# Collecting the second layer's expert results and the double norm behind it: one stage, tile by tile, instead of two

## What is computed

```python
        hn = rms_norm(h, norm_ffn[i])
        h = h + hier_moe(hn, ...)          # sum of two gated expert rows per token
    return rms_norm(h, norm_final)         # end of the first network, x of the second
...
    h, hc = x, ctx
    for layer in range(DEPTH):
        ...
        u = rms_norm_2(h, norm_g[layer]) * (1 + scale) + shift
        uc = rms_norm_2(hc, norm_g[layer]) * (1 + scale_c) + shift_c
```

## Time and profile before

| what | value |
|---|---|
| median of three runs | 3350.32 us |
| profiled execution: device time, span | 3346.29 us, 3344.5 us |
| TensorE busy | 2847.3 us, 85% of the span |
| VectorE, ScalarE, GpSimd busy | 839.7 us (25%), 643.0 (19%), 192.8 (6%) |
| mean granted TensorE clock | 0.949 of 2.4 GHz |
| collecting stage with the context's norm | about 2135.4 to 2154.0 us |
| double norm | 2154.0 to 2185.4 us |
| mixer A's products | 2185.5 to about 2306 us |

### The profile page before, as it was taken

One profiled execution on the slowest core, in us unless ns is written; L12 is line 12 of the kernel. 1 busy time (PEld: TensorE's weight loads), 2 busy tenths in 40 slices (PEclk: granted clock), 3 DMA queues, 4 the chain that ended last, 5 costly groups with the idle time before them and its releaser, 6 DMA issues. The chain is left out here.

```text
span 3344.5 us, 30732 instructions
## 1 busy us (share of the span) xinstructions
PE 2847.3 (85%) x12394; PEld 1426.5 (43%) x12394; DVE 839.7 (25%) x2159; ACT 643.0 (19%) x1388; POOL 192.8 (6%) x144
## 2 busy tenths in 40 slices
PE   7999949778867999998588777489999997999997
PEld 3454533222223444444332222146655564555554
DVE  1130421101102202112211110323714443054044
ACT  2220410000001000001000000213503342142143
POOL 1000010000000000000100000110010102012001
PEclk9999959999998999998699999799999998999999
DMA  5502059999984333224699999701001011121100
GB/s 186 232 26 76 26 216 380 427 427 427 428 335 170 125 115 112 101 75 176 244 428 427 427 427 428 277 25 34 1 27 39 13 51 48 51 73 48 51 23 32
DMA packets 117647, 604.84 MB, mean 181 GB/s; under 512 B 9701, under 2 KB 23978, under 8 KB 92794
## 3 DMA queue, kind: packets, MB, share of 16 engines
q1 hardware_dynamic: 91632, 537.15, 39.8%
q10 hardware_dynamic: 20618, 46.89, 4.0%
q0 software_dynamic: 5248, 18.75, 1.5%
HBM read 559.17 MB, written 43.52 MB: 180 GB/s over the span
## 5 line engine op out<-in xcount | busy, mean ns | idle before, releaser
L479 PE MATMUL psum<-ring,XT 128*128 128x512 f32 (+3 forms) x1216 | 480.2, 555 | 14.7 <-ACT arena L1705 6.6
L469 PE MATMUL psum<-XT,ring 128*128 128x512 f32 (+1 forms) x1152 | 444.2, 547 | 2.8 <-DVEq L2078 2.8
L1061 PE MATMUL psum<-arena 128*64 128x512 f32 x1280 | 306.1, 624 | 114.0 <-DMA arena<-in_expert_w_gu 113.8
L479 PEld LDWEIGHTS psum<-ring,XT 128*128 128x128 f32 x1216 | 230.2, 190 | 256.4 <-issue 222.4
L469 PEld LDWEIGHTS psum<-XT,ring 128*128 128x128 f32 x1152 | 219.3, 191 | 226.8 <-issue 215.6
L561 PE MATMUL psum<-ring,arena 128*128 128x512 f32 x704 | 306.1, 593 | 8.5 <-DVEq L2078 4.2
L1061 PE MATMUL psum<-ring,arena 128*64 128x512 f32 x768 | 191.5, 646 | 70.0 <-DMA ring<-in_expert_w_gu 67.2
L686 PE MATMUL psum<-arena 64*128 64x384 f32 (+8 forms) x704 | 221.1, 500 | 27.1 <-ACT arena L740 22.1
L1061 PEld LDWEIGHTS psum<-arena 128*64 128x64 f32 x1280 | 91.5, 142 | 300.2 <-issue 172.9
L1131 DVE TENSOR_TENSOR arena<-arena,psum 64x512 f32<-64x512 f32 x64 | 44.1, 689 | 692.4 <-ACT arena L1134 692.4
L561 PEld LDWEIGHTS psum<-ring,arena 128*128 128x128 f32 x704 | 132.2, 190 | 171.9 <-issue 159.3
(11 more groups left out here) (246 smaller groups left out, 2323.5 us busy)
## 6 DMA issues: line engine op xcount, KB each, us to landing
arena<-in_expert_w_gu SPq DMA_DIRECT2D x80, 2048.0 KB, 24.7
ring<-in_expert_w_gu SPq DMA_DIRECT2D x48, 2048.0 KB, 24.6
arena<-in_expert_w_down SPq DMA_DIRECT2D x40, 2048.0 KB, 28.1
ring<-in_expert_w_down SPq DMA_DIRECT2D x24, 2048.0 KB, 28.1
ring<-in_ada_w SPq DMA_DIRECT2D x12, 2048.0 KB, 9.3
ring<-in_fox_w_in SPq DMA_DIRECT2D x8, 2048.0 KB, 8.4
arena<-xg_dram ACTq DMA_DIRECT2D x32, 512.0 KB, 10.3
y_dram<-arena ACTq DMA_DIRECT2D x128, 128.0 KB, 8.6
```

The costliest lines, as they stand in the source:

```text
L469: i = pe.matmul(ps[0][0:cols_[1] - cols_[0], 0:ntok], w[:, c, cols_[0]:cols_[1]], x[:, c, tok:tok + ntok], start=(c == 0), stop=(c == k - 1))
L479: i = pe.matmul(ps[0][:, 0:width], x[:, c, t * P:(t + 1) * P], w[:, c, c0:c0 + width], start=(c == 0), stop=(c == k - 1))
L1061: i = pe.matmul(psum[side * BR:(side + 1) * BR, 0:FF], x[:, 4 * part + c, :], w[:, c, side * FF:(side + 1) * FF], start=(part == 0 and c = ...
```

## The change

The two stages become one, `CombineNorms`, for the second layer; the first layer keeps `Combine`. The load of norm_final comes first on ScalarE. VectorE adds a tile's two gathered rows and at once makes its Z; ScalarE takes both sums of squares of each tile as they come, all eight. The roots are as before. TensorE transposes the rows in two passes, tiles 0 and 1 of all banks, then tiles 2 and 3. GpSimd clears mixer A's query halves behind the gathers and then scales H. The places of Z, ROWS, G, the scratch rows and the context's norm in the arena are other ones. Mixer A's products have no clears any more, and a slack towards GpSimd.

```diff
+        class CombineNorms(Combine):
+            Z, ROWS = region(2 * NT * D, NT, D), region(NT * D, NT, D)
+            G, JUNK = region(21504, D), region(22528, D)
+            ZEROS = [region(12288, 8, NTA * P)[(1 - g) * DH:(2 - g) * DH, 4 * g:4 * g + 4, :] for g in range(2)]
...
+            def act(self, act):
+                act.dma_start(self.G, io["norm_final"].partition_broadcast(P)).then_inc(self.s("gain"), 16)
+                self.beside.act(act)
+                for t in range(NT):
+                    act.wait_ge(self.s("summed"), t + 1)
+                    act_step.then(act, act.activation(self.JUNK, H[:, t, :], ACT.Square, accum_out=s2[:, 0, t:t + 1]))
+                    act.wait_ge(self.s("weighted"), t + 1)
+                    i = act.activation(self.JUNK, self.Z[:, t, :], ACT.Square, accum_out=s2[:, 0, NT + t:NT + t + 1])
+                    if t + 1 < NT:
+                        act_step.then(act, i)
+                i.then_inc(self.s("squares"), 1)
...
+            def dve(self, dve):
+                self.beside.dve(dve)
+                dve.wait_ge(self.s("gain"), 16)
+                for t in range(NT):
+                    dve.wait_ge(self.s(f"got{t}"), self.at(f"got{t}") + 32)
+                    for k in range(2):
+                        i = dve.scalar_tensor_tensor(H[:, t, :], self.YG[:, k, t, :], gates[:, k, t:t + 1], H[:, t, :], ALU.mult, ALU.add)
+                        if k == 0:
+                            dve_step.then(dve, i)
+                    i.then_inc(self.s("summed"), 1)
+                    dve.wait_ge(self.s("summed"), t + 1)
+                    dve.tensor_tensor(self.Z[:, t, :], H[:, t, :], self.G, ALU.mult).then_inc(self.s("weighted"), 1)
+                dve.wait_ge(self.s("weighted"), NT)
+                dve.wait_ge(self.s("squares"), 1)
...
+            def pool(self, pool):
+                super().pool(pool)
+                for x in self.ZEROS:
+                    pool_step.then(pool, pool.memset(x, 0.0))
+                pool.wait_ge(self.s("rstd"), 1)
+                for t in range(NT):
+                    pool.tensor_scalar(H[:, t, :], self.Z[:, t, :], s2[:, 1, t:t + 1], None, ALU.mult)
+
+            def pe(self, pe):
+                self.beside.pe(pe)
+                pe.wait_ge(self.beside.s("out_a"), self.beside.at("out_a") + KC)
+                for t0 in range(0, NT, 2):
+                    pe.wait_ge(self.s("rows_a"), t0 // 2 + 1)
+                    pe.wait_ge(self.s("rows_v"), t0 // 2 + 1)
+                    for c in range(KC):
+                        for t in range(t0, t0 + 2):
+                            i = pe.transpose(bank(c)[:, t * P:(t + 1) * P], self.ROWS[:, t, c * P:(c + 1) * P], ident)
+                        if t0 + 2 == NT:
+                            i.then_inc(self.s("turned"), 1)
...
-            combine = Combine(f"cb{layer}")
+            combine = (CombineNorms if layer else Combine)(f"cb{layer}")
             if layer:
                 combine.beside = Norm("m01", HC, D, NCT, lambda c: amod[:, 0, c, 1:2], lambda c: modc[:, 0, c, 1:2], XT, SEQ,
-                                      region(2 * NT * D, NCT, D), side=1, junk=region(2 * NT * D + NCT * D, D)).inline()
+                                      region(18432, NCT, D), side=1, junk=region(18432 + NCT * D, D)).inline()
...
-        class TwoNorms(Stage):
...
-                for t in range(NT):
-                    i = act.activation(self.JUNK[:, 0, :], H[:, t, :], ACT.Square, accum_out=s2[:, 0, t:t + 1])
-                    act_step.then(act, i)
-                for t in range(0, NT, 2):
-                    act.wait_ge(self.s("weighted"), t + 1)
-                    i = act.activation(self.JUNK[:, 0, :], self.Z[:, t, :], ACT.Square, accum_out=s2[:, 0, NT + t:NT + t + 1])
...
-            zeros(p, *(QT[(1 - g) * DH:(2 - g) * DH, 4 * g:4 * g + 4, :] for g in range(2)))
+            p.slack = {(e, "pool"): 1 for e in ("pe", "act", "dve")}
...
-                 lambda: TwoNorms("nfin"), mixer_a, mixer_b,
+                 mixer_a, mixer_b,
```

More of the change, by code:

```diff
@@ L1240, in dve @@
                                                                     H[:, t, :], ALU.mult, ALU.add))
+        class CombineNorms(Combine):
+            Z, ROWS = region(2 * NT * D, NT, D), region(NT * D, NT, D)
+            G, JUNK = region(21504, D), region(22528, D)
+            ZEROS = [region(12288, 8, NTA * P)[(1 - g) * DH:(2 - g) * DH, 4 * g:4 * g + 4, :] for g in range(2)]
+            one, two = slice(0, NT), slice(NT, 2 * NT)
+            def act(self, act):
[9 more added lines that the diff above has]
+                i.then_inc(self.s("squares"), 1)
+                act.wait_ge(self.s("rstd"), 1)
+                for t in range(0, NT, 2):
+                    act.activation(self.ROWS[:, t, :], self.Z[:, t, :], ACT.Copy, scale=s2[:, 3, t:t + 1]).then_inc(self.s("rows_a"), 1)
+                for c in range(0, KC, 2):
+                    act.wait_ge(self.s("turned"), c + 1)
+                    act.activation(XT[:, c, 0:SEQ], bank(c), ACT.Identity, scale=amod[:, 0, c, 0:1], bias=modc[:, 0, c, 0:1])
+            def dve(self, dve):
[12 more added lines that the diff above has]
+                dve.wait_ge(self.s("squares"), 1)
+                dve_step.then(dve, dve.tensor_scalar(s2[:, 0, self.one], s2[:, 0, self.one], 1.0 / D, EPS, ALU.mult, ALU.add))
+                root_of(dve, *(s2[:, j, self.one] for j in (0, 2, 3, 1)))
+                r, ms = s2[:, 1, self.one], s2[:, 0, self.two]
+                dve_step.then(dve, dve.tensor_tensor(s2[:, 2, self.one], r, r, ALU.mult))
+                dve_step.then(dve, dve.tensor_tensor(ms, ms, s2[:, 2, self.one], ALU.mult))
+                dve_step.then(dve, dve.tensor_scalar(ms, ms, 1.0 / D, EPS, ALU.mult, ALU.add))
+                root_of(dve, *(s2[:, j, self.two] for j in (0, 2, 3, 1)))
+                dve.tensor_tensor(s2[:, 3, self.one], r, s2[:, 1, self.two], ALU.mult).then_inc(self.s("rstd"), 1)
+                dve.wait_ge(self.s("rstd"), 1)
+                for t in range(1, NT, 2):
+                    dve.tensor_scalar(self.ROWS[:, t, :], self.Z[:, t, :], s2[:, 3, t:t + 1], None, ALU.mult).then_inc(self.s("rows_v"), 1)
+                for c in range(1, KC, 2):
+                    dve.wait_ge(self.s("turned"), c + 1)
+                    dve.tensor_scalar(XT[:, c, 0:SEQ], bank(c), amod[:, 0, c, 0:1], modc[:, 0, c, 0:1], ALU.mult, ALU.add)
+            def pool(self, pool):
[16 more added lines that the diff above has]
+                            i.then_inc(self.s("turned"), 1)
@@ L1308, in loads @@
             stage.small = 16 * len(pairs)
[L1310 to L1315, removed]
         def gain_cols(at):
```

## The result

The changed kernel takes 3328.92 us in the median of seven runs (3325.95 to 3336.10), the kernel before, beside it, 3347.22 (3342.69 to 3352.61). The ratio is 0.9946, interval 0.9935 to 0.9957: 14 to 22 us faster. The forecast was 3337 with 3331 as the low end, so the way was right and the time lies outside the range.

The account below looks back on a forecast made before the run. The prediction took the two stages as a chain of waits, chiefly 7.35 us for a load and 3.5 for GpSimd. Gains of 8.4, 3.4 and 1.7 us made 13.5, from 3350.3 to 3336.8, said as 3337; range 3331 to 3344.

Parts of the forecast that it names:

- the seam: First gather to mixer A's seventeenth product, all that the change touches; the forecast gain summed to 13.5 us.
- Start of the tile sums: Joined stage: the early gain load pushes the gathers back 0.5 us, so VectorE's first sum starts at 2143.2.
- Tile loop: VectorE in the joined stage: two adds and one product per tile, 3.82 us each, four tiles 15.3 us.
- The end of the roots: End of the joined stage's two roots: 2164.8 instead of 2173.2, 8.4 us earlier.
- Clears beside the adds: GpSimd's two clears beside VectorE's adds in the joined stage: cost taken as 0, upper end 3.4 us.
- Rival B: Joined stage: clears hold VectorE 3.4 us, gathers delayed 1.4 more, clock falls 1.7; gain 7.0 us, 3343; chance 0.16.
- From the roots to the first product: Row scaling, transposes and copies up to mixer A: 8.9 us after the roots instead of 12.3.
- the split: Transposing in two passes of tile pairs ahead of mixer A brings nothing, because the copies to XT bound it.
- The clock at mixer A's start: TensorE's shorter idle gap keeps full clock over mixer A's first products: 1.7 us gained, lower end 0.
- rival C: Mixer A: TensorE's clock stays at 1.2 GHz, losing 25 us, 3363.5, slower; chance 0.03.
- The slack: Mixer A's products may start before GpSimd has finished scaling H: 3.4 us gained.
- Rival D: Something taken as free, such as a weight unit or GpSimd's queue, ends the chain: 3346, within 0.2%; chance 0.07.

Follow-up runs that it names:

- b_gain: The kernel before, two stages kept, with the load of norm_final issued at the head of the collecting stage; 0.9983 against the kernel before.
- a_onepass: The changed kernel with the transposes in one pass of four tiles to a bank, as before; 0.9963 against the kernel before.
- b_warm: The kernel before with 24 more transposes, results unread, on TensorE while GpSimd still scales H; 0.9986 against the kernel before.
- b_slack: The kernel before with mixer A's products given slack towards GpSimd and Z of the double norm moved; 0.9993 against the kernel before.
- b_delay: The kernel before with the first root's product with itself made eleven times, a 2.0 us delay; 1.0003 against the kernel before.
- a_best: The changed kernel with 40 filler transposes ahead of the rows and the first root ahead of Z's squares; 0.9948 against the kernel before.
- a_gainlate: The changed kernel with the load of norm_final issued behind the context's norm on ScalarE; 0.9981 against the kernel before.

## Why the prediction was wrong, and where it was right

The mechanism and nearly all terms of the seam were right; its sum was 13.5, and the traces show 13.9 in the first pair and 13.3 in the means. That these are so near is in part luck, since small misses of both signs cancel.

- *Start of the tile sums*: forecast 2143.2, found 2143.29, released by a gather. The agreement is luck: the forecast put 0.5 us of push by the load on a first gather at 2136.00, and the trace has no push on one at 2136.58. The first sum comes 6.71 us behind the first gather in both. In the changed kernel's two other traces it is 7.35 and 7.78, in b_gain, with the same early load, 6.58, so the push is small, and what else moves the first sum stays open.
- *Tile loop*: 15.3 forecast, 15.2 found (2143.29 to 2158.48). The end of the roots: 2164.8 forecast, 2164.73 found, with the same 0.6 us of later start in it.
- *Clears beside the adds*: taken at 0 with 3.4 as the upper end. Two adds take 2.60 us at 2147.07, under GpSimd's clears, as they do at 2143.29, ahead of them. Rival B falls with it; its two other terms did not come either. The trace agrees here with what was cited of the Trainium skill (SBUF — State Buffer, Who interferes with whom), that a GpSimd instruction which only writes does not hold a VectorE one with two SBUF inputs.
- *From the roots to the first product*: 8.9 forecast, 9.17 found. The transposes ran at 0.50 for 5.6 of their 6.42 us, where I had taken the clock to rise half-way. That the split brings nothing held in the trace (a_onepass).
- *The clock at mixer A's start*: 1.7 forecast and 1.7 found; rival C did not occur in any of the ten traces of the changed seam that kept its slack. b_warm and b_slack show that the idle TensorE was the cause.
- *The slack*, 3.4 forecast: 12.3 less 9.2, 3.1, in the pair; the miss is that of the term above. Rival D did not come.

**The steps that failed** are the last ones. First, "From the median 3350.3: 3336.8". That median of three executions was a poor base: 95 executions of the same kernel have a mean of 3345.4, 4.9 us lower. The profiled execution stood at 3346.3 and I had seen that the two differ by 4.0, but took the higher as the base and used the lower only for the range's edge. From 3345.4 the same sum gives 3331.9. Second, the sum held nothing for the code behind the seam; only the range had "1 for the clock's shorter dips elsewhere falling otherwise". In the profiled pair these dips gave 4.4 us, in the means 1.9 (15.2 less 13.3, with an uncertainty of ± 1.4 on the first alone). The two together (4.9 and 1.9, less 0.2 that the seam gave less than its sum) are 6.6 us, and with the 0.2 by which 3336.8 was rounded up they are the 6.7 by which 3337 missed the mean of 3330.3, and the measured median of 3328.9 lies another 1.4 below that mean.

What stays open is whether the 1.9 belong to the change. For it: all five first traces of two-stage kernels have 1148.2 us and more behind the seam, against at most 1149.6 for the first five of one-stage kernels, and b_delay lost only 0.5 of its 2.0 us. Against it: a_best, one stage, has 1153.3, b_delay, two stages, 1147.8, the means over all traces (1150.9 in six with two stages, 1148.7 in eleven with one) differ by 2.3 us with a standard error of 1.6, and the last column of the table varies from 3283.6 to 3289.9 with no order by seam length or stages. That the dips of the clock carry the differences is shown for the pair, by the two stretches above; that the seam's length steers them was only tried, by three delays, and not shown.

## What to carry to other kernels

Look in a chain of short stages for the transfer that is issued only where it is needed, and for the stage change that waits for an engine whose result is wanted much later; here they were 6.7 and 3.1 us of the seam, and either could be had with an edit of a few lines. When TensorE stands ahead of a long run of products, price the idle time ahead of it too: the gap cost 1.7 us more than its length. And take the base of a small forecast from all executions seen, the profiled one included, with their spread in the range: a sum for the seam that was right to half a microsecond was put on a median of three that stood 4.9 us too high.

## What I had not expected of the hardware

Code that nobody touched differs by up to 10 us: behind the seam the traces ran from 1146.0 to 1155.9 us, with the clock at 0.50 or 1.00 over the same instructions. Most of the difference is TensorE's busy time, 1054.5 to 1062.2 us over the 17 traces; its idle time there was 90.6 to 93.8. Ahead of the seam it is no better: the first gather comes between 2130.3 and 2141.4 us. How much the time scatters is itself uneven: the eleven executions of a_gainlate lie between 3336.9 and 3339.4 us, those of the kernel before beside them between 3339.6 and 3351.1. And a shorter chain need not show: a_best saves 3.3 us of seam in its trace, and its mean of five executions does not show it.
